# Conditioning rows by two rounded products, and other orders at five places, in a stack of six transformer layers

## The chip, the cores and the metric

The kernel runs on one core of one Trainium2 chip. The metric is the device time in microseconds. Every time of the profile comes from one profiled execution, read by the hardware profiler.

## The reference

Two blocks follow each other on 256 rows of 1024 values.

The first block has four layers of the kinds A, B, C, A. Each computes one wide product `x @ w_in` (queries, keys, values, queries for a memory, in kind A an indexer too), rotates queries and keys, attends, multiplies by `w_out`, adds the scaled residual and normalizes, and then does the same round a gated feed-forward of width 2816. Kind A keeps for each query the 64 keys with the highest indexer score; B is dilated attention; C is causal attention. Every layer also attends to 256 memory rows.

The second block has two layers: modulation of normalized rows, retention of four heads, stick-breaking attention of eight heads, and a gated output.

```python
c_act = jax.nn.silu(c.astype(jnp.float32))
mod = c_act @ w_ada + b_ada                      # the conditioning rows: 1024 x 3072 a layer
shift, scale, gate = jnp.split(mod, 3, axis=-1)
h = rms_norm(x, norm_g) * (1.0 + scale[:, None, :]) + shift[:, None, :]
...
_, sel = lax.top_k(score, topk)                  # kind A: 64 of 256 keys
...
log_keep = jnp.where(mask, jax.nn.log_sigmoid(-z), 0.0)
suffix = lax.cumsum(log_keep, axis=3, reverse=True) - log_keep
a = jnp.where(mask, jnp.exp(log_beta + suffix), 0.0)
```

## The kernel before

Each engine runs its own program, and all of them are made from one list of steps, written by the class `Plan`. Each engine goes through the list and emits only the kinds of step it has a function for. So the order of the list is the order of each engine's queue; semaphores join the queues.

**Weights.** They come as 266 tiles of 128x2048 float32 (1 MB) over SyncE's (SP's) queue into three raw buffers. A step `high` lets ScalarE (ACT) copy the tile to a rounded 4-byte format (`w_high`, L1234), a step `low` lets VectorE (DVE) subtract the two and round the rest (`w_low`, L1402). There are five places for such pairs. Every large product is three products in the rounded format: high by high, low by high, high by low (`products`, L911 to L913). Rows are transposed on TensorE (PE), with ACT taking the high half and DVE the low one. `split` emits the low halves due and the next high one; `on` first advances the background work by one slot, then calls `split`; one slot is one group of 12 or 24 products. One low half, at the end of the last feed-forward, is made by GpSimd (POOL) instead: the step `low_aside`, L1902.

**Background work** consists of generators advanced one slot at a time: the rotations, the attention units, the indexer. `indexer_work` yields after each of the first seven rounds of the top-8 search (L1623, L1626) and then writes the mask `select_bias` (L1634). `headed` starts the first attention unit early, and `begun` lets it skip one slot.

**Attention.** `attention` gives the order keys, values of the first 128 rows (`some(0, t, ...)`), the two tail blocks (`t_tail`: block 1 is the memory's queries, transposed, block 0 the last value columns), values of the second rows. The tail's tiles lie ahead of the values' tiles in the stream. `begin` starts the units after the first of these blocks.

**Conditioning rows.** There are 24 tiles `w_ada_2`, two to a row of 512 columns, spread over steps 3 to 8 of the four feed-forwards. DVE multiplies a tile by the conditioning column and adds it up over eight chunks in one of two accumulators `ada_acc` (L1416, L1418), freed by `ada_added`. Then PE sums over partitions: one float32 product with a 128x12 matrix of ones (L1145), which the trace shows as two passes. DVE adds it to the row's place (L1712). In the plan the step `ada` follows directly on `ada_tile`, at the end of a feed-forward step.

**Second block.** `stick_work` runs four pairs of heads through scores, `sb_keep` on DVE (L1799, L1804), `sb_later` on PE (L1189 to L1192) and weighting.

## Time and profile before

| | |
|---|---|
| median of 3 timed runs | 1649.32 us (1649.16 to 1650.0) |
| profiled execution | 1647.88 us |
| its span, first to last instruction | 1646.1 us |
| mean granted clock of TensorE | 0.994 |
| PE busy | 1592.5 us, 97% |
| DVE busy | 1064.5 us, 65% |
| ACT busy | 722.7 us, 44% |
| POOL busy | 53.6 us, 3% |
| chain that ended last | PE 87%, DVE 9%, issue 2% |
| read from memory | 296.20 MB, 182 GB/s over the span |

A busy time is the union of an engine's instructions. Matmuls are pipelined and their ends are modelled, so the starts are read where an exact step matters. PEld is the load of PE's stationary operand, which overlaps PE. In rows of a timeline the columns are start, duration of the merged group, engine, line, operation, output and inputs, shape and count; in brackets stands the idle time of the engine before it and what ended it.

### The profile page before, as it was taken

The page shows a single profiled execution, that of the slowest core. Times are in us where ns is not written, and L with a number is a line of the kernel's source. Part 1 is how long each engine was busy: PE and PEld are TensorE (multiplying, and loading weights), DVE is VectorE, ACT ScalarE, POOL GpSimd, SP SyncE. Part 2 cuts the span into 40 slices and gives each one's busy share as a digit, 9 for nine tenths or more (in the row PEclk, how much of TensorE's full clock was granted, in tenths as well). Part 3 has the DMA queues.
Part 4 walks back from the last instruction along what each step waited for, and adds up shares of the span by engine and source line. Part 5 has one row for each costly group of instructions (what it writes and reads, how often), then busy time and mean ns, then how long its engine had stood idle before and what let it go on. Part 6 is the DMA issues. An engine that isn't in the chain of part 4 may idle for free.

```text
span 1646.1 us, 20172 instructions
## 1 busy us (share of the span) xinstructions
PE 1592.5 (97%) x8388; PEld 1323.8 (80%) x8388; DVE 1064.5 (65%) x1439; ACT 722.7 (44%) x861; POOL 53.6 (3%) x90
## 2 busy tenths in 40 slices
PE   7999999999999999999999999999999989999998
PEld 5898888888878878888888888778888878887976
DVE  5784766647566775575767656847666477556744
ACT  4545444333444433444443443544443334554452
POOL 1100000000000000000000000000100010000000
PEclk9999999999999999999999999999999999999999
DMA  8651466655424766362466644414756536433530
GB/s 267 252 189 69 164 227 235 247 213 179 154 77 166 281 238 247 130 229 78 152 245 233 264 169 164 175 52 151 269 228 250 211 118 228 147 119 124 205 116 26
DMA packets 45035, 299.89 MB, mean 182 GB/s; under 512 B 5444, under 2 KB 5700, under 8 KB 11280
## 3 DMA queue, kind: packets, MB, share of 16 engines
q1 hardware_dynamic: 38736, 278.48, 45.9%
q0 software_dynamic: 5776, 19.01, 3.9%
q8 instruction: 66, 1.08, 0.3%
q10 hardware_dynamic: 432, 1.11, 0.2%
q14 instruction: 25, 0.20, 0.0%
HBM read 296.20 MB, written 2.65 MB: 182 GB/s over the span
## 4 chain that ended last, share of the span: by engine, by line
PE 87%; DVE 9%; issue 2%; DMA 1%; ACT 1%; POOL 0%; SPq 0%; POOLq 0%; DVEq 0%; ACTq 0%
PE psum L911 25%; PE psum L913 25%; PE psum L912 25%; DVE w_low L1402 3%; PE psum L934 3%; PE psum L1125 2%; PE psum L990 2%; PE psum L1137 1%; DMA w_raw<-in_weights 1%; PE psum L1105 1%; PE psum L1051 1%; PE psum L1189 1%; PE psum L1145 1%; DVE arena L1684 1%; DVE work L1743 0%
## 5 line engine op out<-in xcount | busy, mean ns | idle before, releaser
L911 PE MATMUL psum<-w_high,xt_high 128*128 128x512 f32 (+2 forms) x1472 | 576.8, 392 | 16.2 <-DVE w_low L1402 5.0
L1402 DVE TENSOR_TENSOR w_low<-w_raw,w_high 128x2048 fp32r<-128x2048 f32 x240 | 544.9, 2273 | 53.1 <-ACT w_high L1234 52.2
L1234 ACT ACTIVATE w_high<-w_raw 128x2048 fp32r<-128x2048 f32 x241 | 458.8, 1905 | 263.8 <-DMA w_raw<-in_weights 159.4
L913 PE MATMUL psum<-w_high,xt_low 128*128 128x512 f32 (+2 forms) x1472 | 565.8, 384 | 0.0
L912 PE MATMUL psum<-w_low,xt_high 128*128 128x512 f32 (+2 forms) x1472 | 565.0, 384 | 0.0
L911 PEld LDWEIGHTS psum<-w_high,xt_high 128*128 128x128 f32 x1472 | 277.9, 189 | 83.4 <-DVE w_low L1402 10.1
L913 PEld LDWEIGHTS psum<-w_high,xt_low 128*128 128x128 f32 x1472 | 277.9, 189 | 55.8
L912 PEld LDWEIGHTS psum<-w_low,xt_high 128*128 128x128 f32 x1472 | 278.3, 189 | 50.9
L1695 DVE TENSOR_TENSOR arena<-arena,psum 128x256 f32<-128x256 f32 x88 | 37.0, 420 | 216.1 <-ACT arena L1325 215.7
L911 PE MATMUL psum<-w_high,ht_high 128*128 128x512 f32 x352 | 140.9, 400 | 0.0
L913 PE MATMUL psum<-w_high,ht_low 128*128 128x512 f32 x352 | 137.6, 391 | 0.0
L912 PE MATMUL psum<-w_low,ht_high 128*128 128x512 f32 x352 | 137.2, 390 | 0.0
L1325 ACT ACTIVATE arena<-psum 128x256 f32<-128x256 f32 x88 | 33.7, 383 | 231.8 <-PE psum L913 231.8
L1302 ACT ACTIVATE work<-psum,neg_max 128x256 f32<-128x256 f32 (+3 forms) x112 | 49.9, 460 | 72.4 <-DVE neg_max L1651 70.9
L1428 DVE TENSOR_TENSOR xt_low<-psum,xt_high 128x512 fp32r<-128x512 f32 x64 | 42.0, 685 | 55.2 <-ACT xt_high L1242 55.2
L913 PEld LDWEIGHTS psum<-w_high,ht_low 128*128 128x128 f32 x352 | 66.1, 188 | 14.4
L912 PEld LDWEIGHTS psum<-w_low,ht_high 128*128 128x128 f32 x352 | 66.3, 188 | 12.8
L911 PEld LDWEIGHTS psum<-w_high,ht_high 128*128 128x128 f32 x352 | 66.2, 188 | 12.5
L1242 ACT ACTIVATE xt_high<-psum 128x512 fp32r<-128x512 f32 x64 | 36.2, 596 | 79.4 <-PE psum L990 79.0
L1260 ACT ACTIVATE arena<-psum 128x512 f32<-128x512 f32 x48 | 28.6, 595 | 86.2 <-PE psum L913 86.2
L1418 DVE SCALAR_TENSOR_TENSOR arena<-w_raw,c_col,arena 128x512 f32<-128x512 f32 x84 | 63.0, 750 | 2.6
L1897 POOL TENSOR_TENSOR norm_rstd<-norm_rstd,half_neg 128x1 f32<-128x1 f32 (+1 forms) x32 | 19.7, 617 | 1228.9 <-DVE norm_rstd L1472 949.9
(222 smaller groups left out, 1618.0 us busy)
## 6 DMA issues: line engine op xcount, KB each, us to landing
w_raw<-in_weights SPq DMA_DIRECT2D x263, 1024.0 KB, 4.8
norm_params<-in_ln_g POOLq DMA_DIRECT2D x8, 512.0 KB, 4.3
norm_params<-in_ln_b POOLq DMA_DIRECT2D x8, 512.0 KB, 5.8
kv_outside<-arena POOLq DMA_DIRECT2D x3, 512.0 KB, 4.2
mem_kv<-kv_outside POOLq DMA_DIRECT2D x3, 512.0 KB, 3.5
norm_params<-mods_outside POOLq DMA_DIRECT2D x3, 512.0 KB, 5.8
x_rows<-in_x SPq DMA_DIRECT2D x2, 512.0 KB, 9.0
w_raw<-in_weights SPq DMA_DIRECT2D x2, 512.0 KB, 6.4
```

The source lines that it names most:

```text
L911: e.matmul(dst, a_hi, b_hi, start=first, stop=False)
L912: e.matmul(dst, a_hi, b_lo, start=False, stop=False)
L913: return e.matmul(dst, a_lo, b_hi, start=False, stop=last)
L934: m = e.matmul(dst, left, right, start=banks[i] not in banks[:i], stop=banks[i] not in banks[i + 1:])
L1234: e.activation(K.w_hi[:, g % RING, 0:w], K.w_raw[:, r, 0:w], ACT.Copy).then_inc(K.high.hit(t), 1)
L1242: e.activation(hi[:, 4 * j.g:4 * j.g + 4, j.rb * P:j.rb * P + P], psum[:, K.tr.place(j.use), :].rearrange("p (c s) -> p c s", s=P), ACT.Co ...
L1302: m = e.activation(dst, src, ACT.Exp, bias=K.negmax[:, slot, n:n + 1], accum_out=K.expsum[:, slot, n:n + 1])
L1325: e.activation(K.ff_silu[j.step % 2][:, j.rb, :], psum[:, K.gemms.place(j.use), 0:FF_STEP], ACT.Silu).then_inc(K.silu_done.hit((j.layer, j ...
L1402: e.tensor_tensor(K.w_lo[:, s, 0:w], K.w_raw[:, r, 0:w], K.w_hi[:, s, 0:w].bitcast(F32), ALU.subtract).then_inc(K.taken.hit(t), 1)
L1418: m = e.scalar_tensor_tensor(out=acc, in0=w, scalar=c, in1=acc, op0=ALU.mult, op1=ALU.add)
L1428: e.tensor_tensor(lo[at], psum[:, K.tr.place(j.use), :].rearrange("p (c s) -> p c s", s=P), hi[at].bitcast(F32), ALU.subtract).then_inc(K. ...
L1695: e.tensor_tensor(K.ff_h[j.step % 2][:, j.rb, :], K.ff_silu[j.step % 2][:, j.rb, :], bank[:, FF_STEP:BLK], ALU.mult).then_inc(K.gemms.sem( ...
```

## The change

1. The sum over partitions of a conditioning row is made by two products in the rounded format: ACT rounds the accumulator (`ada_halves`, high), DVE subtracts (low), and PE multiplies a 128x128 matrix of ones with each. The matrix lies in a buffer shared with attention, and is set again in each feed-forward. The product is issued after the next step's block.
2. In all four layers the order of `attention` becomes memory's queries, values of the first rows, last value columns, values of the second rows. In layer 1 (kind B) the two tail blocks stood the other way round.
3. The rounds of the top-8 search take five slots in place of eight.
4. In layer 0 the second rows of the first projection are evacuated by ACT, not by DVE.
5. The low half that POOL made goes back to DVE (`low_aside` is gone).
6. In the stick-breaking layers the first pair's `sb_keep` comes one slot earlier (`begun_twice`).

```diff
@@ Plan
         if half:
-            self.ada_use[row], self.ada_tiles[row] = self.tr.take(), t
+            self.ada_tiles[row] = t
+            self.add("ada_halves", row)
+            self.ada_waiting.append(row)
+
+    def ada_row(self):
+        for row in self.ada_waiting:
+            self.ada_use[row] = self.tr.take()
             self.add("ada", Ada(row, self.ada_use[row]))
+        self.ada_waiting = []
@@ indexer_work
-            if n < TOPK // 8 - 1:
+            if n % 2 if n < 6 else n < TOPK // 8 - 1:
                 yield
@@ feed_forward
         for step in range(2, FF_STEPS):
+            if step == 2:
+                self.add("ada_ones", layer)
             self.block("w_gate_up", layer, step, gen, gate(step), "up")
+            self.ada_row()
...
             if rb and layer == LAST:
-                self.low(1)
-                self.low(1, "low_aside")
+                self.low()
                 self.ahead()
@@ first_layer
-            by = ("act", "act" if kind == "A" and c < 3 and (layer or c) else "dve")
+            by = ("act", "act" if kind == "A" and c < 3 else "dve")
@@ attention
-        some(0, t, ("proj", layer, 3), "block", [self.on, begin])
-        first, second = (0, 1) if kind == "B" else (1, 0)
-        some(first, t_tail, ("tail", layer), "tail", [self.on] * 2)
-        some(second, t_tail, ("tail", layer), "tail", [self.on] * 2)
+        some(1, t_tail, ("tail", layer), "tail", [self.on, begin])
+        some(0, t, ("proj", layer, 3), "block", [self.on] * 2)
+        some(0, t_tail, ("tail", layer), "tail", [self.on] * 2)
@@ stick_work, headed
-        return self.headed([self.stick_breaking(layer, n) for n in range(SB_H // 2)], 2)
+        return self.headed([self.stick_breaking(layer, n) for n in range(SB_H // 2)], 2, self.begun_twice)
...
-            units[0] = self.begun(units[0])
+            units[0] = (begun or self.begun)(units[0])
+    def begun_twice(unit):
+        next(unit)
+        yield
+        yield
+        yield from unit
@@ tensor_program
     def ada(j):
         pe.wait_ge(*K.tr.free(j.use))
-        pe.wait_ge(*K.taken.at(plan.ada_tiles[j.row]))
-        pe.wait_ge(*K.ones_set.at(0))
-        m = e.matmul(psum[0:12, K.tr.place(j.use), :], K.ones[:, :], K.ada_acc[j.row % 2], start=True, stop=True)
+        pe.wait_ge(*K.ada_low_made.at(j.row))
+        e.matmul(psum[:, K.tr.place(j.use), :], K.ones[:, :], K.ada_hi[:, :], start=True, stop=False)
+        m = e.matmul(psum[:, K.tr.place(j.use), :], K.ones[:, :], K.ada_lo[:, :], start=False, stop=True)
@@ scalar_program
+    def ada_halves(row):
+        act.wait_ge(*K.taken.at(plan.ada_tiles[row]))
+        if row:
+            act.wait_ge(*K.ada_added.at(row - 1))
+        e.activation(K.ada_hi[:, :], K.ada_acc[row % 2], ACT.Copy).then_inc(K.ada_high_made.hit(row), 1)
@@ vector_program
-    e.memset(K.ones[:, :], 1.0).then_inc(K.ones_set.hit(0), 1)
+    def ada_ones(layer):
+        v.wait_ge(*K.tr.out(plan.units[layer, 1][-1].out))
+        e.memset(K.ones[:, :].bitcast(F32), 1.0)
+
+    def ada_halves(row):
+        v.wait_ge(*K.ada_high_made.at(row))
+        e.tensor_tensor(K.ada_lo[:, :], K.ada_acc[row % 2], K.ada_hi[:, :].bitcast(F32),
+                        ALU.subtract).then_inc(K.ada_low_made.hit(row), 1)
@@ gpsimd_program
-    def low_aside(t):
...
```

## Rows read from the trace of the kernel before

**Rows 1.** The page, part 1: engine, busy time, share of the span, instructions.
```profile
PE 1592.5 (97%) x8388; PEld 1323.8 (80%) x8388; DVE 1064.5 (65%) x1439; ACT 722.7 (44%) x861; POOL 53.6 (3%) x90
```

**Rows 2.** Waits of PE, whole span: us in total, times, longest.
```profile
PE psum L911 <- DVE w_low L1402: 5.0, 5, 1.7
...
PE psum L990 <- DVE work L1743: 4.8, 1, 4.8
...
PE psum L934 <- DVE select_bias L1634: 3.5, 1, 3.5
```

**Rows 3.** Timeline round the sums of conditioning rows 0 and 1.
```profile
270.03 0.48 DVE L1416 TENSOR_SCALAR arena<-w_raw,c_col 128x512 f32<-128x512 f32 x1
...
271.51 0.39 PE L911 MATMUL psum<-w_high,ht_high 128*128 128x512 f32 x1
...
271.96 0.39 PE L913 MATMUL psum<-w_high,ht_low 128*128 128x512 f32 x1
272.28 0.10 PEld L1145 LDWEIGHTS psum<-arena,ones 128*12 128x12 f32 x2 [0.35 <-issue]
272.28 1.03 PE L1145 MATMUL psum<-arena,ones 128*12 128x512 f32 x2
...
273.24 0.50 PE L911 MATMUL psum<-w_high,xt_high 128*128 128x512 f32 x1
...
273.80 0.40 PE L913 MATMUL psum<-w_high,xt_low 128*128 128x512 f32 x1
...
307.09 1.03 PE L1145 MATMUL psum<-arena,ones 128*12 128x512 f32 x2
```

**Rows 4.** The page, part 5: groups of 128x512 work, and a weight load.
```profile
L1428 DVE TENSOR_TENSOR xt_low<-psum,xt_high 128x512 fp32r<-128x512 f32 x64 | 42.0, 685 | 55.2 <-ACT xt_high L1242 55.2
...
L912 PEld LDWEIGHTS psum<-w_low,ht_high 128*128 128x128 f32 x352 | 66.3, 188 | 12.8
...
L1242 ACT ACTIVATE xt_high<-psum 128x512 fp32r<-128x512 f32 x64 | 36.2, 596 | 79.4 <-PE psum L990 79.0
```

**Rows 5.** Timelines of ACT and PE, 41 to 46 us.
```profile
41.88 1.91 ACT L1234 ACTIVATE w_high<-w_raw 128x2048 fp32r<-128x2048 f32 x1 [4.13 <-DMA w_raw<-in_weights]
...
45.04 0.50 PE L911 MATMUL psum<-w_high,xt_high 128*128 128x512 f32 x1 [2.65 <-DVE arena L1531]
```

**Rows 6.** Timeline of PE, layer 0, after the last key transposes.
```profile
129.30 0.50 PE L911 MATMUL psum<-w_high,xt_high 128*128 128x512 f32 x1 [0.77 <-DVE w_low L1402]
```

**Rows 7.** Layer 3: DVE, PE; stretches: busy PE PEld DVE ACT POOL, clock, DMA.
```profile
1051.32 0.62 DVE L1623 MAX8 top<-work 128x8 f32<-128x128 f32 x2
...
1052.50 2.28 DVE L1402 TENSOR_TENSOR w_low<-w_raw,w_high 128x2048 fp32r<-128x2048 f32 x1
...
1056.07 0.26 DVE L1542 TENSOR_TENSOR rope_tmp<-arena,rope_cos 128x96 f32<-128x96 f32 x1
...
1057.35 0.87 PE L1051 MATMUL psum<-ident,arena 128*128 128x128 f32 x6 [1.05 <-DVE arena L1545]
...
1076.42 1.65 PE L934 MATMUL psum<-arena 64*128 64x128 f32 x12 [3.51 <-DVE select_bias L1634]
...
1076.00:1080.00 4.00, 3.58 (x24) 3.39 (x25) 1.86 (x4) 0.10 (x1) 0.00 (x0) 0.50 0.32 133
1080.00:1084.00 4.00, 4.00 (x28) 4.00 (x28) 0.00 (x0) 3.38 (x13) 0.00 (x0) 0.77 0.00 0
```

**Rows 8.** End of the last feed-forward: timelines of POOL, DVE and PE.
```profile
1339.88 4.61 POOL L1902 TENSOR_TENSOR w_low<-w_raw,w_high 128x2048 fp32r<-128x2048 f32 x1 [1.99 <-ACT w_high L1234]
...
1340.17 4.87 DVE L1743 TENSOR_TENSOR work<-work,arena 128x512 f32<-128x512 f32 x1
...
1350.12 2.27 DVE L1402 TENSOR_TENSOR w_low<-w_raw,w_high 128x2048 fp32r<-128x2048 f32 x1
...
1364.19 0.47 PE L911 MATMUL psum<-w_high,xt_high 128*128 128x512 f32 x1 [2.17 <-DVE xt_low L1428]
```

**Rows 9.** Timeline of PE, first stick-breaking layer.
```profile
1430.07 0.59 PE L1189 MATMUL psum<-arena,causal 128*128 128x384 f32 x1 [1.32 <-DVE arena L1804]
```

More of the change, by code:

```diff
@@ L159, in __init__ @@
         self.ada_left = [(s, c, half) for s in range(DEPTH_2) for c in range(6) for half in range(2)]
-        self.background, self.norms, self.ada_use, self.ada_tiles = [], [], {}, {}
+        self.background, self.norms, self.ada_use, self.ada_tiles, self.ada_waiting = [], [], {}, {}, []
         self.rets, self.sticks = {}, {}
@@ L172, in high, with low @@
         self.rounded += 1
-    def low(self, count=None, by="low"):
-        for _ in range(self.rounded if count is None else count):
-            self.add(by)
-            self.rounded -= 1
+    def low(self):
+        for _ in range(self.rounded):
+            self.add("low")
+        self.rounded = 0
     def split(self):
@@ L759, in stick_work, with headed @@
     def stick_work(self, layer):
-        return self.headed([self.stick_breaking(layer, n) for n in range(SB_H // 2)], 2)
-    def headed(self, units, steps):
+        return self.headed([self.stick_breaking(layer, n) for n in range(SB_H // 2)], 2, self.begun_twice)
+    def headed(self, units, steps, begun=None):
         if steps:
             next(units[0])
-            units[0] = self.begun(units[0])
+            units[0] = (begun or self.begun)(units[0])
         for _ in range(steps):
@@ L773, in begun @@
     def begun(unit):
+        yield
+        yield from unit
+    @staticmethod
+    def begun_twice(unit):
+        next(unit)
+        yield
         yield
@@ L895, in number @@
                     done = t + 1
-            elif what in ("low", "low_aside"):
+            elif what == "low":
                 t = next(lows, None)
                 if t is not None:
-                    steps.append((what, t))
+                    steps.append(("low", t))
             else:
@@ L903, in number @@
         self.steps = steps
-        self.aside = [t for what, t in steps if what == "low_aside"]
 def products(e, dst, a_hi, a_lo, b_hi, b_lo, first, last):
@@ L1377, in scalar_program @@
               "dots": dots, "scores": scores, "turn_prob": turn_prob, "gate": gate, "turn_h": turn_h,
-              "rms": rms, "ret_weigh": ret_weigh, "sb_scores": sb_scores,
+              "ada_halves": ada_halves, "rms": rms, "ret_weigh": ret_weigh, "sb_scores": sb_scores,
               "sb_later": sb_later, "final": final}
@@ L1897, in power @@
         e.tensor_tensor(r, r, K.half_neg[:, 0:n], ALU.pow).then_inc(K.inverse_root.hit((key, rb)), 1)
-    def low_aside(t):
-        r, s, w = t % RAW, plan.place[t] % RING, K.width(t)
-        pool.wait_ge(*K.high.at(t))
-        e.tensor_tensor(K.w_lo[:, s, 0:w], K.w_raw[:, r, 0:w], K.w_hi[:, s, 0:w].bitcast(F32),
-                        ALU.subtract).then_inc(K.taken_aside.hit(t), 1)
     def stats(j):
@@ L2026, in __init__ @@
         self.ht_hi, self.ht_lo = [[t[:, n, :, :] for n in range(4)] for t in (ht_hi, ht_lo)]
+        with ExitStack() as scope:
+            scope.enter_context(nc.sbuf_tensor("below_ada", [P, 12288], F32))
+            self.ones = scope.enter_context(nc.sbuf_tensor("ones", [P, P], F32R))
+            self.ada_hi = scope.enter_context(nc.sbuf_tensor("ada_high", [P, BLK], F32R))
+            self.ada_lo = scope.enter_context(nc.sbuf_tensor("ada_low", [P, BLK], F32R))
         arena = sb("arena", [P, 10240])
@@ L2066, in __init__ @@
         self.mods, self.norm_rows = arena[0:12, 8192:8704], arena[0:12, 8704:9216]
-        self.ones = sb("ones", [P, 12])
         self.stats = sb("norm_stats", [P, RB, 4, 6])
@@ L2121, in __init__ @@
         self.cond_silu = signal("cond_silu")
-        self.summed, self.ada_added, self.ones_set = signal("ada_summed"), signal("ada_added"), signal("ones")
+        self.summed, self.ada_added = signal("ada_summed"), signal("ada_added")
+        self.ada_high_made, self.ada_low_made = signal("ada_high"), signal("ada_low")
         self.stepped, self.variance = signal("vector_step"), signal("variance")
```

7 lines of the change are left out of this document (2 added, 5 removed).

## The prediction, made before the result

> **What bounds the kernel now.** I read the page first, then TensorE's waits over the whole span, then the timelines around each edited place. TensorE (PE) is busy 97% of the span [rows 1]. That share alone proves little, because the products overlap one another, so I also took the step from one product's start to the next: two steps of 128x512 products take 271.51 to 271.96, 0.45 us, 0.227 each [rows 3], and the feed-forward stretches run at that step nearly without a hole. So time is won in two ways: by giving PE less to do, or by taking away one of its few waits. Those waits are short and known: 5.0 us for low halves of weights, 4.8 us once for a row of L1743, 3.5 us once for the selection mask [rows 2]. What VectorE (DVE) or ScalarE (ACT) does elsewhere costs nothing unless it ends one of them.
>
> **The sums of the conditioning rows.** Now each of the 12 rows costs PE two passes. Before them the last product starts at 271.96, after them products start at 273.24 and (the third) at 273.80 [rows 3]. Without the sum, that third product would have started three steps after 271.96, at 272.64, so one sum takes 1.16 us of PE. It becomes two products with 512 columns in the rounded format, which I take to run at the 0.227 step of the 128x512 products around them: 0.45 us. Gain 0.70 x 12 = **8.4 us**. Ends of this term: the new pair costs 0.45 at best. The nearest higher price is the last product at each of its 0.39 durations, 0.78 in all, gain 4.5. I take the step, since these operands have the form of thousands of others.
>
> The added work: ACT rounds 128x512 (0.60 by L1242), DVE subtracts (0.69 by L1428) [rows 4], 12 times, and DVE sets the ones four times. It is hidden by the feed-forward stretches, where PE has no wait on either. With the cover gone it would be 1.3 us a row. The wait of PE on the subtraction also costs nothing: the halves are issued at the end of one step, the product only after the next block's four groups of 12 products, 4 x 2.7 = 10.9 us later. Queued behind that product on PE are the transposes of the hidden rows, which were queued there anyway. The later product also holds the accumulator longer. Products of successive rows lie 34.8 us apart, and the accumulator is overwritten two rows on: the sum for row 1 starts at 270.03, so that for row 2 at about 304.8, while row 0's product would then be done by about 284 [rows 3]. 21 us of slack.
>
> Here the Trainium skill speaks against the change. The rows: the two loads of the old 12-column ones take 0.10 us together, one of 128 columns 0.19 [rows 3, 4]. The skill, "TensorE: Matmul & The Clock Gate", section "LDWEIGHTS (loading the stationary operand)", says that a load's time goes with its columns. By that rule the new loads are the dearer ones, and the trace agrees. It also shows such loads lying under the products in front of them; were they in the open, the term would lose 12 x 0.28 us and be 5.0.
>
> **One evacuation from DVE to ACT in layer 0** (first projection, second rows). PE waits 2.65 us until 45.04 for DVE to empty the bank, which DVE does behind a low half. On ACT it stands behind a rounding that waits for its DMA and runs 41.88 to 43.79, so ACT ends it at about 44.4 (0.6 us as the ACT rows above) [rows 5]. Gain **0.6 us**; ends 0 (ACT delayed by its own table load) and 0.7.
>
> **Memory's queries before the values' first products.** In each of the four layers PE stands after the last key transposes for the low half of the values' second tile, as until 129.30 with 0.77 us idle [rows 6]. By the step the loss is 1.02 to 1.11, since the overlap hides a part. The query tiles lie ahead of the value tiles in the stream, so their low halves are ready, and the value tiles get 5.9 us more. Layers 0, 1 and 2: 1.0 + 1.1 + 1.1 = **3.2 us**. The queries' evacuation on DVE now comes ahead of the first score maximum. The scores take PE 1.2 us, the evacuation 0.7, so it is covered; uncovered it would be 0.7 a layer. In layer 1 the first weighting now follows closely on ACT's evacuation of the values (0.6 us), with scores of 1.2 us between: covered. Ends: 0 and 3.3.
>
> **Denser rounds of the top-8 search (layers 0 and 3).** Three slots fewer; the same work on DVE, earlier than what stood between. In layer 0 nothing waits for the mask, but an evacuation of a memory product gets behind the rounds: DVE would reach its end about 0.5 us after PE wants the bank. Cost **0.5 us**, ends 0 and 1.5.
>
> In layer 3 DVE has no idle time, and PE waits for it twice: 1.05 us at 1057.35 for rotated queries, 3.51 us at 1076.42 for the mask [rows 7]. One round is 1.2 us (1051.32 to 1052.50 less a gap), a low half 2.2, a rotation 1.2. In the new order four rounds and the low half stand ahead of the first rotation, two more than now: it ends at about 1059.95 instead of 1057.3, and PE's wait there grows from 1.2 to 3.7 us. Then rounds 5 and 6, rotations to 65.2, a low half, rounds 7 and 8 and the mask (71.1), the last rotation (72.4). PE waits 0.4, 0.6 and 0.9 us on these, ends the queries at 76.0, and starts the scores there without waiting for the mask, which is now five us old; two low halves that stood ahead of the mask stand behind it. The start moves only 0.4 us, with 0.4 us more of PE's work done before it: 0.8.
>
> The clock is the larger part. After the 3.51 us of idleness PE ran at a granted clock of 0.50, the 1.2 GHz level, to 1080, and 0.77 on average to 1084 [rows 7]. That lost about 3.58 x 0.5 + 4 x 0.23 = 2.7 us, with nothing waiting on DVE to hide it. In the new order the long idle stretch is the one at 1060, and a slow clock after it is hidden, as PE waits for rotations there anyway. Following both orders to the second scores gives 1085.9 against 1082.8. Gain **3.1 us**; ends 0.4 and 3.6.
>
> **The low half taken back from POOL.** POOL's subtraction runs 4.61 us from 1339.88, and DVE's addition that starts at 1340.17 takes 4.87 us instead of 0.69 [rows 8]: they exclude one another. PE waits 4.8 us for that row [rows 2]. Without POOL the addition ends at 1340.9, 4.2 us earlier. The skill's "SBUF — State Buffer", section "SBUF: two separate sides", describes an exclusive lock held for the whole instruction; the row agrees, and the sum goes by the row. DVE gets a second low half of 2.2 us (2.27 with its overlap by [rows 8]), and loses 0.6 us of idle time between the two transposed groups. DVE is then busy up to the rows that end PE's next wait, at 1364.19 [rows 8]; what late products cost before that point is hidden in that wait. PE's new waits are 0.6 us for the third tile and 2.2 for the fifth. DVE's next work starts at 1341.0 instead of 1345.0, so the chain arrives 4.0 + 0.6 - 2.2 = **2.4 us** earlier. Ends: 1.5 and 4.2 (if the slow clock after 1364 goes too).
>
> **The first pair's keep-step a slot earlier** in both stick-breaking layers. PE waits 1.32 us at 1430.07 and about as long in the second layer, because DVE has an evacuation ahead of the keep-step [rows 9]. Its input is ready six us before, DVE is idle there, and the two waits go wholly: **2.6 us**; ends 1.9 and 2.6.
>
> **The sum.** 8.4 + 0.6 + 3.2 - 0.5 + 3.1 + 2.4 + 2.6 = 19.8 us. The profiled execution took 1647.9, with a span of 1646.1, so it becomes 1628.1. The median of the timed runs lies 1.4 us above it, which gives **1629.5**, 1.2% less.
>
> **The rivals.**
> (a) The slow clock in layer 3 stays, since a 3.7 us wait takes the place of the 3.5 us one and its aftermath reaches open work. For: the idle time is of the same length. Against: PE waits for DVE directly behind it. 1629.5 + 2.7 = 1632.2.
> (b) The reordered products only move their waits to the evacuation that now stands on DVE before the maximum. For: DVE is the dense engine. Against: the 0.5 us of cover worked out above. The 3.2 us are lost and layer 3 gives 1 less: 1633.7.
> (c) The pair of products costs its higher price, or the 128-column loads stand open. For: the first product after a change of kind takes 0.50 us at 273.24, not 0.39 [rows 3]. Against: the pair is of the same kind as its neighbours. 3.9 or 3.4 us less: 1633.4 or 1632.9.
> (d) More is won: the slow clock after 1364 goes as well, and the 0.5 us in layer 0 doesn't appear: 1629.5 - 2.2 = 1627.3.
> (e) Slower. PE must wait for each row's halves: DVE's sum of a later row waits for the accumulator, holds up the low halves queued behind it, and PE starves. It decides from 19.8 / 12 = 1.65 us a row, which needs the 21 us of slack used up first; at 2 us a row it would be 1653.5.
> (f) The change doesn't do what it says: two rounded products cost PE what the two old passes did. All 8.4 are lost: 1637.9.
>
> **How the numbers follow.** Forecast 55% (its own range 1628 to 1631.2), (a) 18%, (b) 9%, (c) 6%, (d) 8%, (e) 2%, (f) 2%. The range 1626.8 to 1634 holds the forecast, (a) to (d), and leaves out (e), (f) and strays. 0.2%, 3.3 us, is about what can be told from no change. All cases but (e) lie more than that below: faster 0.97, within 0.01, slower 0.02.
>
> **What would show it.** Right: PE's conditioning products start 0.23 us apart with 0.45 us for both, in all 12 rows; no idle time before the query products in four layers; POOL without a subtraction of weights, and the addition beside it at 0.69; no wait at L1189; in layer 3 a long wait before the query transposes, none for the mask, and a granted clock of 1.00 from the scores on. Wrong: waits of PE on L1145's new operands, a clock of 0.50 after the scores, or a wait on DVE's evacuation behind the query products.

## The result and the profile after

| | before | after |
|---|---|---|
| median of the timed runs | 1649.66 us (1649.16 to 1651.81, 4 runs) | 1628.67 us (1627.76 to 1629.48, 4 runs) |
| ratio, 95% interval | | 0.987, 0.9853 to 0.9889 |
| profiled execution | 1647.88 us | 1628.01 us |
| its span | 1646.1 us | 1626.2 us |

1629.5 us were predicted. The profiled time fell by 19.9 us; the terms had summed to 19.8. The experiments below show that this agreement is better than the terms deserve: in three places the slow level of TensorE's clock (1.2 GHz, a granted clock of 0.50) moved about, for and against.

Line numbers of after: the products of weights L925 to L927, the pair L1158 and L1159, transposes L1065, scores L948, low half L1421, addition L1771. Part 1 of the page of after, which answers to [rows 1]:

```profile
PE 1583.9 (97%) x8388; PEld 1327.8 (82%) x8388; DVE 1069.6 (66%) x1454; ACT 728.7 (45%) x874; POOL 48.9 (3%) x89
```

DVE and ACT do a little more, PE 8.6 us less. PE's waits over the whole span of after, against [rows 2]:

```profile
PE psum L925 <- DVE w_low L1421: 4.0, 3, 1.9
PE psum L1065 <- DVE arena L1564: 3.6, 1, 3.6
...
PE psum L1004 <- DVE work L1771: 0.7, 1, 0.7
```

The 4.8 us for one row are 0.7, the wait for the mask is gone, and 3.6 us for rotated queries are new. The timeline of PE in after round the first pair, against [rows 3]:

```profile
281.03 0.39 PE L927 MATMUL psum<-w_high,xt_low 128*128 128x512 f32 x1
281.26 0.39 PE L1158 MATMUL psum<-ada_high,ones 128*128 128x512 f32 x1
281.49 0.39 PE L1159 MATMUL psum<-ada_low,ones 128*128 128x512 f32 x1
281.71 0.60 PE L1151 MATMUL psum<-ident,arena 128*128 128x128 f32 x4
```

From start to start the pair takes 281.26 to 281.71, 0.45 us; the twelve pairs take 0.456 to 0.459 by the unrounded starts. PE in layers 0 and 3 of after, against [rows 5] and [rows 7]:

```profile
44.14 0.50 PE L925 MATMUL psum<-w_high,xt_high 128*128 128x512 f32 x1 [2.04 <-ACT arena L1274]
...
1050.64 1.54 PE L1065 MATMUL psum<-ident,arena 128*128 128x128 f32 x6 [3.65 <-DVE arena L1564]
...
1067.98 0.94 PE L948 MATMUL psum<-arena 64*128 64x128 f32 x12
```

The evacuation's wait is 2.04 us in place of 2.65, 0.6 us shorter. In layer 3 the long wait stands before the query transposes and the scores at 1067.98 wait for nothing. The same stretch in windows, columns as in [rows 7]:

```profile
1050.00:1056.00 6.00, 5.36 (x16) 4.49 (x17) 5.64 (x28) 0.87 (x2) 0.00 (x0) 0.50 0.15 64
...
1066.00:1070.00 4.00, 4.00 (x40) 3.61 (x39) 3.25 (x3) 0.00 (x0) 0.00 (x0) 1.00 0.79 281
```

The slow clock came behind the moved wait, and from the scores on it is 1.00. Both were forecast.

**Where the time went.** The same transposes of rows occur in every kernel, so their starts cut each trace into comparable stretches. The table gives for each stretch the length minus that in the first profile of before, in us; the start times in the first column are those of before. Every column is one profiled execution.

| stretch | before, 2nd | after | after, 3rd | sums alone | POOL's half back | old product order | old rounds, layer 3 | sum forms | last version |
|---|---|---|---|---|---|---|---|---|---|
| start to 62 | +0.7 | -0.9 | +0.1 | +1.0 | -1.3 | +0.5 | -1.1 | -1.4 | +0.3 |
| 62 to 212, layer 0 attention | -0.1 | -0.7 | -0.7 | 0.0 | -0.7 | +0.4 | -0.7 | -0.7 | -0.7 |
| four feed-forwards | +0.1 | -9.0 | -8.9 | -8.7 | -9.0 | -9.0 | -9.0 | -5.0 | -8.8 |
| 403 to 475, layer 1 | -0.2 | -1.3 | -1.3 | -0.1 | -1.4 | -0.1 | -1.3 | -1.3 | -1.3 |
| 475 to 488, layer 1 | +1.6 | +1.6 | +1.4 | 0.0 | +1.5 | 0.0 | +1.6 | 0.0 | +1.5 |
| 710 to 824, layer 2 | -0.1 | -1.2 | -0.9 | -0.1 | -1.1 | -0.1 | -1.1 | -1.2 | -1.1 |
| 1015 to 1159, layer 3 | -0.9 | -1.9 | -3.0 | -2.4 | -2.8 | -0.8 | +0.5 | -3.2 | -5.3 |
| 1340 to 1463 | +1.7 | -5.2 | -3.8 | -2.0 | -1.3 | -3.8 | -5.4 | -3.8 | -5.2 |
| 1489 to 1509 | 0.0 | 0.0 | 0.0 | 0.0 | 0.0 | 0.0 | 0.0 | 0.0 | -1.7 |
| 1509 to 1609 | -0.1 | -1.3 | -1.2 | 0.0 | -1.3 | -1.3 | -1.4 | -1.3 | -1.3 |

The stretches left out agree within 0.2 us. Most rows repeat within 0.3 us wherever the code is the same; a second profile of after lies within 0.2 us of the first in every row. Four rows do not repeat across the kernels: the start, 475 to 488, layer 3 and 1340 to 1463. In the last three it is the clock.

### The profile page after: what moved, and what is told of

It is laid out like the page before. It is cut to its first block, busy times and chain, and to the rows that moved or that the text cites. A ratio compares the mean times of both kernels' runs of the same rounds, so it can differ in the third digit from the quotient of the medians.

```text
span 1626.2 us, 20209 instructions
## 1 busy us (share of the span) xinstructions
PE 1583.9 (97%) x8388; PEld 1327.8 (82%) x8388; DVE 1069.6 (66%) x1454; ACT 728.7 (45%) x874; POOL 48.9 (3%) x89
## 3 DMA queue, kind: packets, MB, share of 16 engines
q8 instruction: 66, 1.08, 0.3%
HBM read 296.20 MB, written 2.65 MB: 184 GB/s over the span
## 4 chain that ended last, share of the span: by engine, by line
PE 87%; DVE 8%; issue 2%; DMA 2%; ACT 1%; POOL 0%; SPq 0%; POOLq 0%; DVEq 0%; ACTq 0%
PE psum L925 25%; PE psum L927 25%; PE psum L926 25%; DVE w_low L1421 3%; PE psum L948 3%; PE psum L1139 2%; PE psum L1004 2%; DMA w_raw<-in_weights 2%; PE psum L1151 1%; PE psum L1065 1%; PE psum L1119 1%; PE psum L1203 1%; DVE arena L1703 1%; DVE work L1645 0%; DVE top L1642 0%
## 5 line engine op out<-in xcount | busy, mean ns | idle before, releaser
L925 PE MATMUL psum<-w_high,xt_high 128*128 128x512 f32 (+2 forms) x1472 | 576.5, 392 | 13.8 <-DVE w_low L1421 4.0
L1421 DVE TENSOR_TENSOR w_low<-w_raw,w_high 128x2048 fp32r<-128x2048 f32 x241 | 546.6, 2271 | 51.0 <-ACT w_high L1248 49.6
L927 PE MATMUL psum<-w_high,xt_low 128*128 128x512 f32 (+2 forms) x1472 | 566.7, 385 | 0.0
L925 PEld LDWEIGHTS psum<-w_high,xt_high 128*128 128x128 f32 x1472 | 278.7, 189 | 71.2 <-DVE w_low L1421 6.3
L927 PEld LDWEIGHTS psum<-w_high,xt_low 128*128 128x128 f32 x1472 | 278.4, 189 | 55.9
L925 PE MATMUL psum<-w_high,ht_high 128*128 128x512 f32 x352 | 140.8, 400 | 0.0
L927 PE MATMUL psum<-w_high,ht_low 128*128 128x512 f32 x352 | 137.5, 391 | 0.0
L927 PEld LDWEIGHTS psum<-w_high,ht_low 128*128 128x128 f32 x352 | 66.1, 188 | 14.3
L925 PEld LDWEIGHTS psum<-w_high,ht_high 128*128 128x128 f32 x352 | 66.2, 188 | 12.5
L1670 DVE TENSOR_REDUCE neg_max<-psum 128x4 f32<-128x1024 f32 (+3 forms) x31 | 32.6, 1052 | 39.0 <-PE psum L948 39.0
```

What stands on the lines that cost most here:

```text
L925: e.matmul(dst, a_hi, b_hi, start=first, stop=False)
L927: return e.matmul(dst, a_lo, b_hi, start=False, stop=last)
L1421: e.tensor_tensor(K.w_lo[:, s, 0:w], K.w_raw[:, r, 0:w], K.w_hi[:, s, 0:w].bitcast(F32), ALU.subtract).then_inc(K.taken.hit(t), 1)
```

## The experiments

All ran beside the kernel before. Its median was 1649.0 us (1646.42 to 1651.7) in the first session, 1649.73, 1648.03 and 1648.48 in the others.

### The sums alone

The kernel before with the first part of the change alone (its `ada_halves`, `ada_ones` and `ada_row` included):

```diff
...
-        m = e.matmul(psum[0:12, K.tr.place(j.use), :], K.ones[:, :], K.ada_acc[j.row % 2], start=True, stop=True)
...
+        e.matmul(psum[:, K.tr.place(j.use), :], K.ones[:, :], K.ada_hi[:, :], start=True, stop=False)
+        m = e.matmul(psum[:, K.tr.place(j.use), :], K.ones[:, :], K.ada_lo[:, :], start=False, stop=True)
```

> The kernel before with the first part of the change alone: conditioning rows summed by two rounded products, issued a block later; all other orders, POOL's low half and the evacuation as before. Theory: the two products cost two steps of 0.227 us and the transition into the following transposes costs nothing more, so the distance from one row's sum to the next falls from 34.81 to 34.06 us as in the changed kernel, 0.75 x 12 = 9.0 us: 1649.7 - 9.0 = 1640.7. By the forecast's own term (0.70 a row) it would be 1641.3. Rival: a share of what the feed-forward stretches gained came from the other parts of the change (fewer low halves waiting, another state on entry): then 1642 to 1644. Rival: the later wait for the halves costs something that the rest of the change hides: PE would show waits on the new operands. The long waits of before (row of POOL's lock 4.8, mask 3.5, keep-step 1.3 twice) all stay.

1640.18 us (1635.73 to 1642.35, 6 runs), ratio 0.9942 (0.9929 to 0.9956). The four feed-forwards give 8.7 us, and PE waits for none of the new halves. So the first part is worth its full amount by itself. The profiled execution was the fastest of the six, 1635.73 us, and layer 3, where the code is that of before, was 2.4 us shorter. PE's waits there, 1040 to 1075 us:

```profile
PE psum L951 <- DVE select_bias L1656: 3.5, 1, 3.5
PE psum L1068 <- DVE arena L1567: 1.1, 1, 1.1
```

The waits are those of before, to the tenth. The windows round the end of the mask's wait say what differs:

```profile
1068.00:1072.00 4.00, 1.21 (x19) 1.11 (x19) 3.18 (x15) 0.00 (x0) 0.00 (x0) 1.00 0.81 293
1072.00:1076.00 4.00, 4.00 (x37) 4.00 (x34) 0.96 (x1) 2.74 (x10) 0.00 (x0) 1.00 0.00 0
```

1.00 where the first profile of before had 0.50 and 0.77 [rows 7]. So the same wait is not always followed by the slow clock, which I had counted as if it were. It is no rare chance either: the second profile of before, below, has 3.4 us of it there.

### POOL's half restored

```diff
-                self.low()
+                self.low(1)
+                self.low(1, "low_aside")
                 self.ahead()
...
```

> The changed kernel with one part undone: the second low half at the end of the last feed-forward is made by POOL again. Theory: POOL's subtraction and DVE's addition exclude one another again (4.6 and 4.9 us instead of 4.6 and 0.69), PE waits about 4.8 us for that row, and the stretch up to the next projection, 3.9 us shorter in the changed kernel, is long again: 1628.7 + 3.9 = 1632.6. The forecast's term was 2.4: 1631.1. Rival: what was gained beyond 2.4 is a slow clock after the next wait, which comes and goes by the moment at which the wait falls and not by its length: then 1631.1 with a granted clock of 1.00 in the projection after that wait, or 1632.6 with 0.5 there; the windows of the profile tell which.

1629.98 us (1629.32 to 1630.61), ratio 0.9884 (0.9871 to 0.9896). POOL's subtraction takes 4.62 us again and PE waits 4.83 us. 1340 to 1463 is 3.9 us longer than in after. But the rival's sign is there too, the window behind PE's next wait:

```profile
1350.00:1354.00 4.00, 4.00 (x13) 2.99 (x12) 2.09 (x6) 0.00 (x0) 0.00 (x0) 0.58 0.92 350
```

So the 3.9 us are the part's own gain and a slow stretch. The third profile of after has that slow stretch too (0.60 in 1348 to 1352) and lies at -3.8; against it POOL's half costs 2.5 us, the 2.4 of the forecast. The timed median is only 1.3 us above that of after, less than the theory's 3.9 and the 2.4 of the forecast's term. The size of the part therefore rests on the stretches; the start alone differs by more than that between executions (-1.3 here, +0.1 in the third profile of after).

### The old order of the products

```diff
-        some(1, t_tail, ("tail", layer), "tail", [self.on, begin])
-        some(0, t, ("proj", layer, 3), "block", [self.on] * 2)
-        some(0, t_tail, ("tail", layer), "tail", [self.on] * 2)
+        some(0, t, ("proj", layer, 3), "block", [self.on, begin])
+        first, second = (0, 1) if kind == "B" else (1, 0)
+        some(first, t_tail, ("tail", layer), "tail", [self.on] * 2)
+        some(second, t_tail, ("tail", layer), "tail", [self.on] * 2)
```

> The changed kernel with one part undone: the old order of the products in all four layers' attention (values of the first rows before memory's queries; in layer 1 the other order of the tail blocks). Theory: a wait for the low half of the values' second tile is back in each of the layers 0, 1, 2 (1.0 to 1.2 us each by the distances of the two traces): 1628.7 + 3.3 = 1632.0 if the new slow stretch of TensorE's clock in layer 1 (3.4 us at 0.50, 1.6 us lost) stays, 1630.4 if it goes. Rival, the new order brings that slow stretch by what it puts ahead of it: it goes here, and the net is 1630.4. Against this rival: PE's wait ahead of it, 1.9 us for probabilities, was there before too, at a clock of 1.00. Rival (b) of the forecast, the waits only moved: 1628.7.

1633.64 us (1631.92 to 1635.5), ratio 0.9906 (0.9893 to 0.9919), more than either expectation. The table shows 1.0 to 1.2 us lost in each of the layers 0, 1 and 2 and, which I had not counted apart, 1.1 in layer 3 (with 6.8 us of slow clock in both kernels), 4.3 in all. The wait of [rows 6] is back, in layer 0 of this kernel:

```profile
130.16 0.50 PE L926 MATMUL psum<-w_high,xt_high 128*128 128x512 f32 x1 [0.77 <-DVE w_low L1422]
```

The slow stretch in layer 1 was absent, which favoured the rival that the new order brings it. The second profile of the kernel before and the run with three forms of the sum, both below, show that it can come with the old order and stay away with the new one.

### The old rounds in layer 3

```diff
-            if n % 2 if n < 6 else n < TOPK // 8 - 1:
+            if (n % 2 if n < 6 and layer != LAST else n < TOPK // 8 - 1):
```

> The changed kernel with one part undone: in layer 3 the rounds of the top-8 search take eight slots again (layer 0 keeps five). Theory: PE's wait ahead of the query transposes falls from 3.8 to about 1.2 us, the wait of 3.5 us for the mask ahead of the scores returns, and with it a clock of 0.50 that hits products and scores nobody waits for; layer 3 gave 1.9 us by the distances of the two traces where 3.1 were forecast: 1628.7 + 1.9 = 1630.6 (by the forecast's term 1631.8). Rival: the 1.9 us come from the order of the products and not from the rounds, whose wait only moved from the mask to the queries: 1628.7.

1630.16 us (1628.58 to 1631.27), ratio 0.9884 (0.9869 to 0.9899). PE's waits, 1040 to 1075 us:

```profile
PE psum L948 <- DVE select_bias L1653: 4.9, 1, 4.9
PE psum L1065 <- DVE arena L1564: 1.0, 1, 1.0
```

The mask's wait is back and longer than before's 3.5 us. The wait of 0.77 us for a low half ahead of it, which sums alone still has, is gone, so PE reaches the mask sooner and waits there 1.4 us longer. From 1066 on, 7 us follow at a mean clock of 0.53. Layer 3 is 2.4 us longer than in after, the timed median 1.5. Layer 3 now stands in all four combinations, each with 6.8 us of slow clock: 0 with both orders old, -0.8 with the new rounds alone, +0.5 with the new product order alone and -1.9 with both. The gains don't add up: with the old rounds the mask is the last to arrive, and what the product order saves ahead of it is lost in waiting for it.

### Both kernels once more

> The changed kernel once more, unaltered, for a second profile. In the profiles so far PE ran at a granted clock of 0.50 in some stretches of 3.4 or 6.8 us behind a wait, and not in the others, though the waits are the same. Theory: which wait is followed by a slow stretch differs between executions of one kernel; then this profile has its slow stretches elsewhere than at 479.5, 1049.5 and 1343.1 us (at least one of the three gone or another added), and the distances between the same instructions outside such stretches agree within 0.1 us. Rival: the order of the instructions fixes it (the three kernels with the new order of the products in layer 1 had a slow stretch at about 479, the three with the old order none): then all three are here again, at the same places.

> The kernel before once more, unaltered, for a second profile. Its first profile had a granted clock of 0.50 in 1075.0 to 1081.8, 1344.6 to 1348.1 and 1365.1 to 1368.5 us; the kernel with the sums alone, the same there, had none at the first and third of these and gained 2.4 and 1.9 us in these places. Theory: the slow stretches come and go between executions, so that layer 3 takes 2.4 us less here if the first is gone, and there is none or another in layer 1. Rival: they are fixed by the order of the instructions: the same three are here.

> The changed kernel unaltered for a third profile. The second one had its slow stretches of TensorE's clock at the same three places as the first, against what was expected; but the two profiles of the kernel before differ in theirs (one at 485.9 and one at 45.5 us more), and one kernel with the same work in layer 1 had none there. Theory: they differ between executions, and the first two profiles of this kernel agreed by chance; here at least one of 479.5, 1049.5 (6.8 us long) and 1343.1 is gone, shorter, or another is added. Rival: for this kernel they are fixed: all three again.

The second profile of after (1627.96 us) was its first again, slow stretches and all: my theory missed. That of before (1650.58) was not like its first. At the three places of the first it had slow stretches again, in layer 3 of 3.4 us in place of 6.8 (that layer is 0.9 us shorter, not the 2.4 of my theory), and three more, from 45.5, 485.9 and 1431.4 us. Windows of before, first profile:

```profile
480.00:484.00 4.00, 2.82 (x19) 1.96 (x17) 3.92 (x6) 2.79 (x3) 0.00 (x0) 1.00 0.00 0
484.00:488.00 4.00, 3.26 (x16) 2.70 (x17) 2.38 (x5) 1.93 (x8) 0.00 (x0) 1.00 0.75 262
```

and of its second profile, at the same work:

```profile
481.50:485.50 4.00, 2.08 (x15) 1.42 (x14) 3.97 (x7) 2.79 (x3) 0.00 (x0) 1.00 0.25 33
485.50:489.50 4.00, 4.00 (x12) 3.12 (x11) 1.30 (x3) 1.93 (x8) 0.00 (x0) 0.57 0.54 229
```

In both PE waits 1.92 us for probabilities ahead of it. One execution goes on at full clock, the other at the 1.2 GHz level for 3.4 us, which costs 1.6 us. And the kernel with the three sum forms, which has the new order, had 1.00 there. So the order doesn't decide it alone. Whether it makes it likelier is open: nine of ten profiles with the new order have this stretch, and one of four with the old one. In the third profile of after (1629.75 us) the slow stretch of layer 3 lasted 3.4 us, not 6.8, and the one at 1343 was gone, with another at 1348.8 and one at 44.9: the expected difference between executions. What decides it in one execution was not isolated. Over all fourteen profiles a slow stretch came behind layer 3's wait of 3.5 to 4.9 us in ten of twelve, and in neither of the two (the last version and the one before it) in which no wait there is longer than 1.3 us.

### Three forms of the sum

```diff
+        kind = j.row % 3
+        if kind == 0:
...
+        elif kind == 1:
+            m = e.matmul(psum[:, K.tr.place(j.use), :], K.ones[:, :].bitcast(F32), K.ada_acc[j.row % 2], start=True, stop=True)
+        else:
+            m = e.matmul(psum[0:12, K.tr.place(j.use), :], K.ones[:, 0:12].bitcast(F32), K.ada_acc[j.row % 2], start=True, stop=True)
```

> The changed kernel with three forms of the sum over partitions, one per row of each feed-forward, all at the new place behind the next block: the first row as changed (two rounded products with 128 columns of ones), the second one float32 product with 128 columns, the third one float32 product with 12 columns (the old form). Theory: a float32 product of 512 columns is two passes of 0.44 and 0.52 us whatever the number of its columns, and the old form at the new place costs about what it cost at the old one, 1.1 to 1.2 us: both float32 rows 0.6 to 0.75 us dearer than the first. Rival, the place matters: the old form costs clearly less here (0.9 or less), since transposes follow in place of rounded products. Rival, the columns matter: the second row is dearer than the third by what two loads of 128 columns last longer than two of 12, about 0.28 us.

1629.97 us, one run. All matmuls and loads on the lines of the two float32 forms (columns: ns min/median/max, first and last start); 128 columns:

```profile
L1163 PEld LDWEIGHTS psum<-arena,ones x8: 187/188/188, 314.5 to 1251.7; 128*128 128x128 f32 x8
L1163 PE MATMUL psum<-arena,ones x8: 590/590/591, 314.7 to 1252.2; 128*128 128x512 f32 x8
```

12 columns:

```profile
L1165 PEld LDWEIGHTS psum<-arena,ones x8: 89/91/93, 349.3 to 1286.3; 128*12 128x12 f32 x8
L1165 PE MATMUL psum<-arena,ones x8: 592/596/600, 349.3 to 1286.7; 128*12 128x512 f32 x8
```

The durations hide it; the timeline of PE shows it. 128 columns:

```profile
314.51 0.39 PE L927 MATMUL psum<-w_high,xt_low 128*128 128x512 f32 x1
314.74 1.02 PE L1163 MATMUL psum<-arena,ones 128*128 128x512 f32 x2
315.59 0.60 PE L1151 MATMUL psum<-ident,arena 128*128 128x128 f32 x4
```

12 columns:

```profile
348.98 0.39 PE L927 MATMUL psum<-w_high,xt_low 128*128 128x512 f32 x1
349.30 1.03 PE L1165 MATMUL psum<-arena,ones 128*12 128x512 f32 x2
350.26 0.66 PE L1151 MATMUL psum<-ident,arena 128*128 128x128 f32 x4
```

From the product before to the transposes it is 1.08 and 1.28 us, against 0.68 for the rounded pair. Up to the first product behind the transposes it is 1.44, 1.69 and 1.04. So against the pair a float32 sum costs 0.40 more with 128 columns and 0.65 with 12: the narrow form is 0.25 us **dearer**, the reverse of the last rival, though its loads are half as long. The theory held for the narrow form alone: at the new place it costs 1.10 us (0.65 and the pair's 0.45), so the place is not what matters most. By the stretches the eight float32 sums cost 4.0 us more than pairs (-5.0 against -9.0), 0.50 each, and by these steps 0.52. It starts 0.32 behind its predecessor, not 0.23, and its second pass takes 0.52, not 0.43. The Trainium skill, "TensorEngine Tiling (Array Packing)", section "Key Properties", says that a change of the tiling mode drains the engine; the profile labels this form 128*12 and all around it 128*128. The 0.25 us would agree with such a drain at both ends; whether twelve columns count as another mode, no run here shows.

### Two better orders

```diff
-            if n % 2 if n < 6 else n < TOPK // 8 - 1:
+            if (n < 4 if layer == LAST else n % 2 if n < 6 else n < TOPK // 8 - 1):
@@ first() of the output projection
-            self.split()
             added(0)
             self.xt(mix, 1)
+            self.split()
```

> The changed kernel with two more orders. (1) In layer 3 the rounds of the top-8 search take their slots as one, one, one, one and four (layer 0 stays): the rotations of the first queries and keys come 2.5 and 3.7 us earlier on DVE, the mask at the same moment as now (it had 6 us to spare). Theory: PE's wait ahead of the query transposes falls from 3.8 to 1.2 us, and 1.4 us of it are kept, up to the rotation of the last keys, which can't come earlier than all eight rounds; ends 0 and 2.4. (2) In the second block's output projection the first gated addition goes ahead of the low half that now stands before it on DVE: the waits of 1.1 and 0.7 us for the additions in the first of the two layers go, 1.8 us. Together 1628.7 - 3.2 = 1625.5. Rival: the late rounds hold the mask back past the scores' need, since PE arrives earlier: a wait for the mask of 1 to 2 us is back and (1) gives nothing: 1626.9. Rival: the low half behind the addition is late for its own product: 0.5 to 1 us less.

1629.34 us (1628.03 to 1631.0), ratio 0.987 (0.9852 to 0.9889): 1625.5 were expected, and nothing is gained on after. PE's waits, 1040 to 1075 us:

```profile
PE psum L1065 <- DVE arena L1564: 4.7, 2, 3.6
```

1.05 us of it is for the queries, as expected, and a new 3.6 us for the last keys, behind four rounds in one slot; I had guarded only the mask. The additions' waits stayed as they were, 1.5 us in all, since the low half is issued a hook earlier than the line I moved.

The next run is again the changed kernel with two orders; the move in `first()` shown above stays in it.

```diff
-            if n % 2 if n < 6 else n < TOPK // 8 - 1:
+            if (n < 4 or n == 6 if layer == LAST else n % 2 if n < 6 else n < TOPK // 8 - 1):
@@ hooks of the output projection's first rows
-                   [[self.split, self.split, first, second], [self.split, self.split, turned, last]], True)
+                   [[self.split, self.ahead, first, second], [self.split, self.split, turned, last]], True)
```

> The changed kernel with two orders, after what the run before it showed: there PE's wait for the queries fell to 1.2 us, and a wait of 3.8 us for the rotation of the last keys came, because four rounds of the search stood ahead of it; and the low half had not moved behind the first gated addition, as it is issued one hook earlier. (1) Layer 3's rounds now take their slots as one, one, one, one, three and one: the last round and the mask stand behind the last keys' rotation and its low half. Theory: the round is 1.25 us and the mask 1.2, so the rotation is ready 2.4 us earlier than there, about when PE wants it, and the scores wait at most 0.5 us for the mask: layer 3 takes 2.0 us less than in the changed kernel (ends 1 and 2.6). Rival, VectorE's dense work sets the end in any order: the wait appears once more in another place (for the last keys or for the mask), and layer 3 keeps its length within 0.5 us. (2) The low half really behind the first addition: both waits of 1.1 and 0.7 us go, 1.8 us (rival: the low half is late for its product, and 0.5 to 1 us of it come back). Together 1628.7 - 3.8 = 1624.9; with the rival of (1) 1626.9.

1626.78 us (1624.83 to 1627.86), ratio 0.9868 (0.9849 to 0.9887). Layer 3 came right: 5.3 us shorter than in before and 2.1 shorter than the new orders without a slow stretch (-3.2). The second part went wrong. PE's waits, 1465 to 1485 us, after and then this kernel:

```profile
PE psum L925 <- DVE work L1856: 1.5, 2, 0.9
```

```profile
PE psum L925 <- DVE work L1856: 2.1, 1, 2.1
```

These waits are for the second rows' additions, and I had moved the first rows'; the deferred low half only made DVE's queue ahead of them longer. PE waits 0.6 us more, and a slow stretch from 1473.2 us (a granted clock of 0.57 in 1473 to 1477) takes most of the rest of the 1.9 us by which 1489 to 1509 is longer.

The last version keeps those rounds, takes both other edits back and moves the second rows' additions:

```diff
@@ turned(), last() of the output projection, first of the two layers
-            self.low()
...
+                added(2)
                 self.xt(("sin", layer + 1), 0)
+                self.low()
...
+            self.add("add_gated", late[3])
             self.split()
-            added(3)
+            self.add("rms", (layer + 1, 1))
...
```

> The changed kernel with two orders. (1) In layer 3 the rounds of the search take their slots as one, one, one, one, three and one, as in the run before, where layer 3 took 2.1 us less than an undisturbed layer 3 of the changed kernel: again 2.1 us (0.3 to 0.5 for the mask and 1.4 for the last keys are left of the waits). (2) The run before put the wrong additions ahead: the waits of 1.1 and 0.7 us at 1474 and 1478 us are for the second rows' additions, behind two low halves, and delaying a low half of the first rows made one wait of 2.3 us of them. Now the second rows' additions go ahead of the low halves due there: theory, both waits fall under 0.2 us and the stretch between the two layers of the second block is 1.8 us shorter. Rival: the low halves behind them come late and hold up the transposed rows or the fourth product instead, 1 us or more of it comes back, or the second rows' norm is late for its transposes at 1490 us. Together 1628.7 - 3.9 = 1624.8; with the rival 1626 to 1627.

**1624.58 us** (1624.44 to 1626.24, 4 runs), ratio 0.9859 (0.9842 to 0.9875). Each of its four runs is below each of after's (1627.76 and up). PE's waits, 1040 to 1075 us:

```profile
PE psum L1070 <- DVE arena L1569: 2.3, 2, 1.3
PE psum L1070 <- ACT arena L1289: 0.5, 1, 0.5
PE psum L953 <- DVE select_bias L1658: 0.2, 1, 0.2
```

3.6 us have become 2.5 (the 0.5 us for ACT are in after too), there is no slow stretch in layer 3, and from 1465 to 1485 us PE waits for nothing. 1489 to 1509 is 1.65 us shorter.

### Three small parts undone

```diff
-            by = ("act", "act" if kind == "A" and c < 3 else "dve")
+            by = ("act", "act" if kind == "A" and c < 3 and (layer or c) else "dve")
-            if n % 2 if n < 6 else n < TOPK // 8 - 1:
+            if (n % 2 if n < 6 and layer else n < TOPK // 8 - 1):
-        return self.headed([self.stick_breaking(layer, n) for n in range(SB_H // 2)], 2, self.begun_twice)
+        return self.headed([self.stick_breaking(layer, n) for n in range(SB_H // 2)], 2)
```

> The changed kernel with three small parts undone, far enough from each other that each is read in its own stretch: the evacuation in layer 0's first projection is VectorE's again, layer 0's rounds of the search take eight slots again, the first keep-step of the stick-breaking layers comes a slot later. Theory, by the forecast's terms: PE's wait around 42 us is 0.6 us longer; layer 0's attention stretch is 0.3 to 0.5 us shorter than in the changed kernel; each of the two stick-breaking layers is 1.3 us longer: 1628.0 + 0.6 - 0.4 + 2.6 = 1630.8. Rival: the keep-step's wait had gone for another reason (a shift of what stood around it by the low half at 1340), then at most 0.5 us in the first of the two layers. Slow stretches of the clock may add or take 1.5 us each.

1635.44 us, one run. PE's timeline in it:

```profile
44.55 0.79 PE L925 MATMUL psum<-w_high,xt_high 128*128 128x512 f32 x1 [2.65 <-DVE arena L1550]
...
1415.89 1.33 PE L1203 MATMUL psum<-arena,causal 128*128 128x384 f32 x2 [1.32 <-DVE arena L1832]
```

2.65 for 2.04 us; layer 0's stretch at -1.1 where after has -0.7; 1509 to 1609 at 0.0 where after has -1.3; the first keep-step's wait at its old 1.32. All three terms hold by the stretches. The time is 4.6 us above the expected 1630.8; slow stretches came at 44.1, 1351.4 and 1416.2 us as well. 1340 to 1463 lies at -0.8, 4.5 us longer than in after, of which 1.3 is the keep-step.

## Why the prediction was right, term by term

- **Sums: 8.4 predicted, 9.0 measured.** The pair costs the step taken for it. Mis-sized was what goes: rows follow at 34.06 us, not 34.81, so 0.75 each. By the three forms, 0.40 of it is the rounded format and 0.25 the width of 128 columns. The remaining 0.10 is what the new place leaves by subtraction; no run changes the place alone. My upper end was 8.4, so the measured value lay outside. My comparison of the loads was too favourable to the narrow form: [rows 3] show two loads that overlap, and one alone takes 0.09 us, half of the wide one's 0.19.
- **Evacuation: 0.6, measured 0.6.**
- **Memory's queries: 3.2 for three layers, measured 1.0 to 1.1 in layer 0, 1.1 to 1.3 in layer 1 and 1.1 to 1.2 in layer 2.** DVE's evacuation behind the query products ended no wait. Layer 3 gives 1.1 more, but only together with the new rounds; I had it in another term.
- **Rounds, layer 0: -0.5, measured -0.4.**
- **Layer 3: 3.1 predicted, 1.9 measured in the profile.** Mechanism and place came true, down to the 3.65 us wait (3.7). The failed step is "The clock is the larger part". Without slow stretches layer 3 lies at -2.4 with the old orders (sums alone) and at -3.2 with the new ones (sum forms), so the orders themselves give 0.8, the size worked out there. The slow clock cost before's profile 2.4 us, near the 2.7 taken, but that is what one execution lost: the second profile lost 1.5, sums alone nothing behind the same wait. And "a slow clock after it is hidden" was half right: 6.8 us of it behind the moved wait cost 1.3 (-1.9 against -3.2), so rival (a) held by half.
- **POOL's low half: 2.4 predicted.** 1340 to 1463 gives 5.2, of which 1.3 is the keep-step, so 3.9. Free of slow clock behind the next wait, the old code lies at -2.0 (sums alone) and the new at -5.4: 3.4 less 1.3 is 2.1; with it in both, 2.5. The term was sized right by the stretches, though not by the timed runs (1.3), and the other 1.4 to 1.8 us are the slow stretch after 1364 of [rows 8], rival (d)'s, which both profiles of before had and the first two of after had not, but the third had.
- **Keep-step: 2.6, measured 1.3 twice:** in the second layer by its stretch, in the first by the wait of 1.32 us that comes back when it is undone.
- **Not in the sum:** 1.6 us lost to a slow stretch in layer 1. The sum has no term for it.

The clock's entries are +2.4 and +1.9 (1340 to 1463, sums alone) from before's profile, -1.3, -1.6 and -0.1 (same stretch, -5.2 against -5.4) from after's: 1.3 us net of 19.9. The parts themselves are worth about 18.5, less than the 19.8 forecast. Most terms were right, layer 3's was 2.3 us too high without the clock, and it was luck that the clock brought the sum within 0.1 us of the profile.

The timed runs show that the clock is not all chance. The kernel before has 32 runs beside the experiments, with a mean of 1648.8 us at a mean granted clock of 0.9934; the changed kernel has six, 1628.7 us at 0.9947. Among runs at the same clock the difference is 17.9 us (0.995, four runs each) or 18.4 (0.994, eight and two), which agrees with the 18.5 for the parts. The other 2 us or so come from a clock that is slow less often in the changed kernel. Which part brings that, no run isolates.

Rivals (b), (c), (e) and (f) fell: no wait on the queries' evacuation, none on the halves, a pair at its step. Of (d) the clock half came in two of three profiles of after, and the other half did not, since layer 0 lost its 0.4 us.

## What to carry to other kernels

Cut two traces at the same instructions and compare stretches before crediting a part; and profile both kernels more than once, since a slow clock behind a wait may come in one execution and not in the next. Compare the mean clocks of many timed runs before calling it chance. Undo interacting orders in all combinations: in layer 3 the product order gained 1.1 us with one layout of the rounds and nothing with the other. Price an instruction by the steps from start to start around it, neighbours included: a narrow stationary operand looks cheaper by its load and was dearer by 0.25 us. When a dense engine feeds several waits, spread its work so that each lands just ahead of its deadline; here the layouts of the same eight rounds set layer 3 up to 5.8 us apart, slow clock included.

## What the hardware showed that was not expected

- The same wait of 1.92 us in layer 1 was followed by a granted clock of 0.50 in some executions and 1.00 in others of the same kernel. Such stretches (those at the kernel's end left out) lasted 3.4 or 6.8 us, came behind waits of 1.0 to 4.9 us, and cost up to 1.7 us per 3.4 us, or 0.3 where the next wait hid the rest (-3.0 against -3.2 in layer 3).
- A float32 product of 512 columns is two passes of 0.43 us, from start to start, with 128 stationary columns, and of 0.44 and 0.52 us with 12, which also starts 0.09 us later behind its predecessor.
- The stretch up to 62 us varied by 3.7 us (-1.4 to +2.3) between profiles of kernels that are alike there, with weights arriving over DMA and slow stretches at 17 to 24 us or near 45 us in some.
